# A two-layer decoder trunk in fp32: the output projection as seven block products instead of eight

## The reference, cut to what matters

```
h = rms_norm(x, norm1_g) * (1 + sc1) + sh1
y_a, y_b = two branches of h @ w_in (state-space mixer, latent attention)
merged = sigmoid(gate_a) * y_a + sigmoid(gate_b) * y_b
x = x + g1 * (merged @ w_out)              # the output projection: 1024 x 1024 x 1024
h = rms_norm(x, norm2_g) * (1 + sc2) + sh2
x = x + g2 * ((silu(h @ w_gate) * (h @ w_up)) @ w_down)
```

## Time and profile before

| what | us |
|---|---|
| median of 3 runs | 2896.54 (2896.39 to 2897.36) |
| the profiled execution | 2895.48 |
| its span, first to last instruction | 2893.6 |
| merge, layer 0 | 649 to 725 |
| output projection, layer 0 | 725 to 814 |
| down projection, layer 0 | 1247 to 1466 |

### The profile page before, as it was taken

How to read it: one execution, slowest core, us unless ns; L and a number is a source line. 1 busy time by engine, 2 the same in 40 slices (tenths; PEclk the granted TensorE clock), 3 DMA queues, 4 the chain that set the end, 5 groups by cost and what they waited for, 6 DMA issues and landing times.

```text
span 2893.6 us, 38026 instructions
## 1 busy us (share of the span) xinstructions
PE 2829.5 (98%) x13924; PEld 2386.9 (82%) x13924; DVE 2103.5 (73%) x2575; ACT 1223.9 (42%) x1965; POOL 1253.3 (43%) x834
## 2 busy tenths in 40 slices
PE   6999999999999999999999999999999899999998
PEld 6888889988877888888878888898888788888887
DVE  7998688865687777757668896788533878776665
ACT  3433377762242333344542335778313333233443
POOL 0354322242535555554625452223223555555454
PEclk9999999999999999999999999999999999999999
DMA  7565400224615544466635652011351345544665
GB/s 293 166 195 177 152 16 13 51 50 155 223 51 192 169 170 164 153 199 217 198 131 160 186 177 74 17 23 41 106 175 44 122 158 174 180 163 155 196 196 167
DMA packets 332745, 408.59 MB, mean 141 GB/s; under 512 B 52369, under 2 KB 242961, under 8 KB 328338
## 3 DMA queue, kind: packets, MB, share of 16 engines
q1 hardware_dynamic: 290128, 298.41, 34.0%
q10 hardware_dynamic: 42434, 107.77, 10.0%
HBM read 299.33 MB, written 104.40 MB: 140 GB/s over the span
## 4 chain that ended last, share of the span: by engine, by line
PE 86%; DVE 6%; ACT 3%; DMA 2%; POOL 1%; issue 1%; SPq 0%; ACTq 0%; DVEq 0%; POOLq 0%
PE ps L709 15%; PE ps L711 15%; PE ps L712 15%; PE ps L1775 9%; PE ps L1777 9%; PE ps L1776 9%; PE ps L1635 4%; PE ps L1616 2%; PE ps L1656 2%; PE ps L1655 2%; PE ps L1621 2%; PE ps L1620 2%; DMA raw<-in_w_b_out 1%; DVE h_lo L2581 1%; DMA ada_rows<-in_w_ada 1%
## 5 line engine op out<-in xcount | busy, mean ns | idle before, releaser
L655 POOL TENSOR_TENSOR wlo<-blocks,whi 128x512 fp32r<-128x512 f32 x288 | 430.3, 1501 | 378.0 <-ACT whi L649 375.2
L693 POOL TENSOR_TENSOR wlo<-raw,whi 128x1024 fp32r<-128x1024 f32 (+4 forms) x156 | 236.4, 1532 | 706.3 <-ACT whi L685 706.2
L649 ACT ACTIVATE whi<-blocks 128x512 fp32r<-128x512 f32 x288 | 180.4, 627 | 316.9 <-PE ps L1777 254.1
L2441 DVE TENSOR_TENSOR d_hi_lo<-blocks,d_hi_lo 128x512 fp32r<-128x512 f32 x154 | 204.3, 1330 | 140.7 <-ACT d_hi_lo L1912 140.4
L666 POOL TENSOR_TENSOR d_hi_lo<-w_pair,d_hi_lo 128x512 fp32r<-128x512 f32 x148 | 203.4, 1377 | 199.4 <-ACT d_hi_lo L1912 199.4
L709 PE MATMUL ps<-h_hi,whi 128*128 128x512 f32 x832 | 281.6, 401 | 7.0 <-DVE h_lo L2581 5.5
L711 PE MATMUL ps<-h_lo,whi 128*128 128x512 f32 x832 | 274.5, 393 | 0.0
L712 PE MATMUL ps<-h_hi,wlo 128*128 128x512 f32 x832 | 273.4, 391 | 0.0
L685 ACT ACTIVATE whi<-raw 128x1024 fp32r<-128x1024 f32 (+4 forms) x162 | 106.9, 699 | 353.0 <-PE ps L712 292.3
L1775 PE MATMUL ps<-h_hi,whi 128*128 128x512 f32 x640 | 249.5, 390 | 5.3 <-issue 3.2
L1777 PE MATMUL ps<-h_hi,wlo 128*128 128x512 f32 x640 | 249.1, 389 | 0.0
(11 more groups left out here) (338 smaller groups left out, 6888.4 us busy)
## 6 DMA issues: line engine op xcount, KB each, us to landing
blocks<-hidden_scratch SPq DMA_DIRECT2D x154, 256.0 KB, 3.7
ada_raw<-in_w_ada SPq DMA_DIRECT2D x64, 512.0 KB, 4.2
raw<-in_w_in SPq DMA_DIRECT2D x92, 256.0 KB, 4.6
w_pair<-in_w_down SPq DMA_DIRECT2D x22, 1024.0 KB, 6.2
sums_scratch<-w_pair ACTq DMA_DIRECT2D x22, 1024.0 KB, 3.9
w_pair<-sums_scratch SPq DMA_DIRECT2D x88, 256.0 KB, 3.3
blocks<-in_w_gate SPq DMA_DIRECT2D x84, 256.0 KB, 3.2
blocks<-in_w_up SPq DMA_DIRECT2D x84, 256.0 KB, 3.0
```

Of the source, the lines that this page charges most:

```text
L649: act.activation(block_view(whi, s), blocks[:, r, :], ACT.Copy).then_inc(block_hi.sem, 1)
L655: pool.tensor_tensor(block_view(wlo, s), blocks[:, r, :], block_view(whi, s).bitcast(F32), ALU.subtract)\
L693: last = pool.tensor_tensor(dst(wlo[:, s, :]), src(raw[:, s, :]), dst(whi[:, s, :].bitcast(F32)), ALU.subtract)
L2441: return dve.tensor_tensor(out, value, hi.bitcast(F32), ALU.subtract)
```

## The change

w_out and the merged input are cut into 2x2 blocks (four pairs of 128 rows, j = 0 to 3) and seven products P1 to P7 of sums of blocks give the result. There are 28 steps (n = 4 p + j, product p in the order P1, P5, P6, P3, P7, P2, P4), each of 4 x 3 matmuls into 4 PSUM banks; products alternate between banks 0 to 3 and 4 to 7. Four of them go on accumulating on what is left in their banks, and after every product DVE adds the 4 banks times g1 to x_sb (28 additions of 128x512 in all). High and low parts go through rings of three slots, as in the down projection. The sums of weight blocks (4 per pair, `weight_sums`) and of input blocks are made on DVE in the merge; w_out's pairs are loaded in its first four tiles. The squares' sum of half 0 is partly on DVE (k = 5 to 7). The 16 products for the modulation rows go into the down projection of layer 0, one every three steps, with their loads.

```diff
+    OPAIRS = KT // 2
+    OSTEPS = 7 * OPAIRS
+    OUT = ("P1", "P5", "P6", "P3", "P7", "P2", "P4")
+    OUT_BANK = {"P1": 0, "P6": 0, "P7": 0, "P4": 0, "P5": 4, "P3": 4, "P2": 4}
+    OUT_OPENS = ("P1", "P5", "P2")
...
# SP: w_out's pairs behind the gates of tiles 0 to 3; after the merge's last loads four plain blocks into raw
+                    if t < OPAIRS:
+                        load_out_pair(t)
...
+                for j in range(OPAIRS):
+                    if j % 2 == 0:
+                        sp.wait_ge(w_lo_done.sem, w_lo_done.at(l, U_MERGE + KT - 1 + j // 2))
+                        apart(sp)
+                    load_out_block(j, 0, 0, raw_part(j))
...
# SP, down projection
+                    if l + 1 < DEPTH and n % 3 == 0 and 0 <= n // 3 - 3 < 2 * KT:
+                        at = n // 3 - 3
+                        load_ada(l + 1, at // KT, at % KT, ada_used.at(l, 4 * KT + at - 1), next_raw)
...
# POOL
+                for n in range(OSTEPS):
+                    pool.wait_ge(wo_hi.sem, wo_hi.at(l, wo_hi_number(n, 0)))
+                    pool.tensor_tensor(ow_tile(n, 1), out_weight(n), ow_tile(n, 0).bitcast(F32), ALU.subtract)\
+                        .then_inc(wo_lo_w.sem, 1)
+                    if 21 <= n < 25:
+                        add_squares(l, 1, 0, n - 20)
+                    if n == 25:
+                        split_lo(pool, l, U_FFN)
+                split_lo(pool, l, U_FFN + 1)
+                for k in range(1, KT):
+                    add_squares(l, 1, 1, k)
...
# PE
+                    if j == 0:
+                        if p < 2:
+                            wait(pe, mg_free, l, KT - 1 + p)
+                        else:
+                            pe.wait_ge(wo_ev.sem, wo_ev.at(l, 4 * (p - 1)))
+                    pe.wait_ge(wo_lo_w.sem, wo_lo_w.at(l, n + 1))
...
+                        if n == 6 * OPAIRS and m == 1:
+                            pe.wait_ge(wo_ev.sem, wo_ev.at(l, 20 + 3))
+                            mean_squares(l, 2)
+                for n in range(OSTEPS):
+                    out_step(n)
+                    if n == 6 * OPAIRS:
+                        norm_scale(l, 2)
...
# ACT
+                def wo_hi_part(n):
+                    if n < OPAIRS:
+                        act.wait_ge(wo_loaded.sem, wo_loaded.at(l, 2 * 16 * OPAIRS))
+                        wait(act, unit_used, l, U_MERGE + KT - 1 + n // 2)
...
+                    else:
+                        act.wait_ge(wo_used.sem, wo_used.at(l, n - 2))
...
+                    copy(ow_tile(n, 0), out_weight(n)).then_inc(wo_hi.sem, 1)
+                    if n >= OPAIRS:
+                        copy(oh_tile(n, 0), out_hidden(n)).then_inc(wo_hi.sem, 1)
...
+                for n in range(2, 27):
+                    wo_hi_part(n)
+                    if 19 <= n < 23:
+                        out_square(0, n - 19)
+                    if n in (23, 24):
+                        for k in range(2):
+                            out_square(0, 2 * (n - 21) + k)
+                    if n == 25:
+                        split_hi(act, l, U_FFN)
                 norm_std(l, 2)
+                wo_hi_part(27)
...
# DVE
+                OUT_EVICTIONS = {8: ((0, 0), (0, 1)), 9: ((0, 2), (0, 3)), 11: ((1, 0),), 12: ((1, 1),), 13: ((1, 2), (1, 3)),
+                                 14: ((2, 0),), 15: ((2, 1),), 16: ((2, 2),), 17: ((2, 3),),
+                                 18: ((3, 0),), 19: ((3, 1),), 20: ((3, 2),), 21: ((3, 3),),
+                                 22: ((4, 0), (4, 1)), 23: ((4, 2), (4, 3))}
...
+                for n in range(OPAIRS, OSTEPS - 2):
+                    out_hidden_low(n)
+                    if n in (8, 11):
+                        wait(dve, x_back[n // 11], l, 16)
+                    for p, m in OUT_EVICTIONS.get(n, ()):
+                        out_eviction(p, m)
+                    if n == 24:
+                        squares_added(0, 5)
+                squares_added(0, 6)
+                squares_added(0, 7)
+                for m in range(4):
+                    out_eviction(5, m, True)
+                out_hidden_low(OSTEPS - 2)
                 norm_inverse(l, 2)
+                out_hidden_low(OSTEPS - 1)
...
+                for k in range(2):
                     hidden_lo(l, 2, k)
+                for m in range(4):
+                    out_eviction(6, m, True)
...
# DVE, down projection
+                    if l + 1 < DEPTH and n >= ADA_STEPS and n % 3 == 0 and n < ADA_STEPS + 6 * KT:
+                        at = (n - ADA_STEPS) // 3
+                        ada_product(l, 4 * KT + at, at // KT, next_raw, next_c)
```

More of the change, by code:

```diff
@@ L1112, in load_down_hidden @@
                     sp.dma_start(blocks[:, n % 4, :], hidden_dram[j, :, at, :]).then_inc(d_loaded[n % 4].sem, 16)
-                sp.wait_ge(s_max.sem, s_max.at(l, 16 * PAIRS))
-                apart(sp)
[L1116 to L1136, removed]
+                sp.wait_ge(wo_loaded.sem, wo_loaded.at(l, 16 * OPAIRS))
@@ new lines, in _ @@
+                sp.wait_ge(mg_comb.sem, mg_comb.at(l, 4 * OPAIRS))
+                apart(sp)
+                for j in range(OPAIRS):
+                    load_out_block(j, 1, 1, out_a22[j // 2][:, j % 2, :])
+                for n in range(2):
+                    sp.wait_ge(wo_lo_w.sem, wo_lo_w.at(l, 5 * OPAIRS + 2 * n + 2))
+                    apart(sp)
+                    up_unit(n)
+                sp.wait_ge(wo_lo_w.sem, wo_lo_w.at(l, 3 * OPAIRS + 4))
+                apart(sp)
+                for name in PLAIN_BLOCKS:
+                    load_block(name, 1)
@@ L1727, in _ @@
                     end[1].then_inc(unit_used.sem, 1)
[L1729 to L1749, removed]
@@ new lines, in out_square @@
+                def out_square(t, k):
+                    act.wait_ge(wo_ev.sem, wo_ev.at(l, (12, 20)[t] + k + 1))
+                    square(l, 1, t, k)
+                for t in range(KT):
+                    if t + 2 < KT:
+                        split_hi(act, l, U_MERGE + t + 2)
+                    if t % 2 == 0:
+                        act.wait_ge(mg_step.sem, mg_step.at(l, 2 * t + 2))
+                        copy(mg_hi[:, t // 2, :], m_sum[:, HALF:SEQ]).then_inc(mg_hi_done.sem, 1)
@@ L2243, in _ @@
+                table(ACT.Sqrt)
+                for n in range(2):
+                    wo_hi_part(n)
+                wait(act, unit_used, l, U_MERGE + KT)
                 wait(act, x_spilled, l, 16)
-                for part, tiles in enumerate((slice(0, 2), slice(2, KT))):
+                for part, tiles in enumerate((slice(0, 4), slice(4, KT))):
                     act.dma_start(x_sb[:, tiles, :], xs_dram[:, tiles, :]).then_inc(x_back[part].sem, 16)
-                for n in range(KT - 2):
-                    split_hi(act, l, U_OUT + n + 2)
-                    wait(act, wo_ev, l, n + 1)
-                    if n == 0:
-                        for part in x_back:
-                            wait(act, part, l, 16)
-                    for t in range(2):
-                        square(l, 1, t, n)
@@ L2255, in _ @@
-                for n in (KT - 2, KT - 1):
-                    wait(act, wo_ev, l, n + 1)
-                    square(l, 1, 0, n)
-                table(ACT.Sqrt)
-                norm_std(l, 2)
-                split_hi(act, l, U_FFN)
-                wait(act, wo_ev, l, KT + 1)
-                square(l, 1, 1, KT - 2)
-                for k in range(3):
-                    hidden_hi(l, 2, k)
-                split_hi(act, l, U_FFN + 1)
-                wait(act, wo_ev, l, KT + 2)
-                square(l, 1, 1, KT - 1)
@@ L2268, in _ @@
[L2268 to L2269 removed]
+                for n in range(2, 27):
+                    wo_hi_part(n)
+                    if 19 <= n < 23:
[5 more added lines that the diff above has]
+                        split_hi(act, l, U_FFN)
+                norm_std(l, 2)
+                wo_hi_part(27)
```

305 lines of the change are left out of this document (203 added, 102 removed).

## The result

The changed kernel takes **2927.55 us** (median of 4 runs, 2926.69 to 2928.93). The kernel before, run beside it, takes 2896.95 (2896.39 to 2900.53). The ratio is **1.0103**, with a 95% interval of 1.0086 to 1.0121: slower by about 1%, where 2921 and slower was forecast, with 2893 to 2934 as the range.

A forecast was written before the change was run, and what follows sets the result against it. PE was taken to bound the kernel, with feeding engines costing nothing if in time. Terms summed to +11.6 us a layer, with the rows 24.7 on 2895.48, and 1.06 for the median: 2921 us, range 2893 to 2934.

The forecast's parts named there:

- gain: Projection: 48 fewer matmuls a layer at 0.2267 us each, 10.9 us a layer saved on PE's path.
- start: Merge to projection: step 0 waits for loads, ACT's copy and POOL's subtraction; +1.5 us a layer (0.5 to 2.5).
- step 4: Projection's step 4 waits for DVE's list behind the last merge tile, colliding with POOL; +1.9 us a layer (0 to 3).
- evictions: Projection steps 8, 12, 16, 20 wait for DVE's evictions of the banks they add to; +5.1 us a layer.
- step 24: Projection: PE's sum of squares waits for squares, adds and P2's evictions; +10.1 us a layer (5.2 to 10.5).
- clock: After PE's idle time in step 24: lower granted clock; +0.9 us a layer (0 to 1.7).
- end: Projection's end to use of half 1's norm: four evictions, squares and adds remain; +3.0 us a layer (1 to 4.5).
- The modulation rows: Layer 0's down projection: 16 added DVE products make PE wait; +1.5 us, once (0 to 3.7).
- The loads: DMA share rises to about 0.8 in the merge and 0.9 in layer 0's down projection; no time cost.
- the first (no collisions): Feeding engines: all DVE operations take 0.68 us, remaining waits eat the gain; 2893 us, chance 0.12.
- the third (half of the wait): Step 24: POOL reaches its adds earlier, wait 5 for 10.1 us, no lost clock; 2909 us, chance 0.17.
- The second, that the gain arrives: Projection: the 28 steps run like the down projection, sum of squares waits under 2 us; 2879 us, chance 0.09.

The follow-up runs named there:

- y1_unit_between: Changed kernel with POOL's long low part of the next stage's first weights moved between weight parts 26 and 27; 2920.3 us, ratio 1.0080 to the kernel before.
- the reordered kernel: Changed kernel with DVE, POOL and ACT lists reordered, evictions and weight sums earlier, six adds a layer moved from POOL to DVE; 2880.9 us, ratio 0.9945.

## Why the prediction was right, term by term

The direction, the mechanism and its place were right; the total of one layer, +11.6, was 3.9 too small, and that of the program 24.7 for 33.5 on the span. Measured by distances of starts in layer 0:

| term | forecast | measured | from |
|---|---|---|---|
| gain | -10.9 | -10.9 | 13828 matmuls for 13924, 48 fewer a layer, at 0.2267 |
| start | +1.5 | +2.25 | 727.17 to 724.92 |
| step 4 | +1.9 | +1.9 | 12.81 - 10.88 |
| evictions | +5.1 | +4.8 | 12.38, 12.41, 11.76, 11.77, less 10.88 each |
| step 24 | +10.1 | +10.1 | 810.68 - (788.30 + 10.88 + 1.36) |
| clock | +0.9 | +2.8 | below |
| end | +3.0 | +4.5 | 15.54 - 11.01; 1.3 of it is the clock once more |

Their sum is 15.5, and 15.46 was measured. All rows but the gain and the clock are distances along one chain, so the agreement checks these two alone.

*Step 24* came as worked out, down to its parts. Behind the start of the step (799.36) the copies for step 25 were forecast at +2.4 and began at +2.35 (801.71). The low part was to end at +5.0 and ended at +4.9. The last add: +9.5, and +9.3. Two experiments take it apart. Moving POOL's long operation takes 2.15 us out of the wait, moving its adds 3.5, each as worked out beforehand.

*Evictions and step 4* were right in cause as well, since moving the evictions or the sums alone removes these waits. Step 4 was to cost 1.9 us by four operations that collide, of the seven between the last tile's sum and the low part; five did (1.67 to 1.78 each), since POOL's parts ended at 737.4 for 735.5. That the 1.9 agrees is luck: step 4 began at 739.98 for 739.2, and step 0, from which it is counted, at 727.17 for 726.4.

*The clock* was the largest mis-sized term. I took the 0.72 over 6 us of the earlier trace rows, behind a shorter pause. Here it was 0.52 over 5.8 us. The sum of squares took 1.72 us to the next start for 0.81 before, six matmuls 2.71 for 1.36, the norm 1.38 for 0.81: 0.9 + 1.35 + 0.6 = 2.8, above the upper end (1.7) that I had given. And I had the clock fall once; it fell again behind the wait for half 1's sum. From that sum to the norm's first use it took 4.95 us (835.14 to 840.09) at a granted 0.67, where y1_unit_between took 3.66 at 1.00 in its layer 0. These 1.3 us are in the row of the end, so the clock cost 4.1 us a layer for 0.9: this is the term that was mis-sized. The Trainium skill (TensorE: Matmul & The Clock Gate, "What's actually happening") has the clock fall with an idle PE: the trace agrees, since without the pause (squares left out) the sum in step 24 takes 1.05 again.

*The end* was at the upper bound (4.5); without the clock it is 3.2, for 3.0. POOL's six adds took 1.63 each (9.78), near the 1.77 taken. But the order of the turns there has two outcomes: the kernel with the long operation between parts 26 and 27 had an end of 13.0 us in one layer and of 15.0 in the other. Counted from the sum in step 24, the first use came 27.85 and 29.10 us later there, and 1.0 of these 1.25 is the clock between half 1's sum and the use (windows of that stretch in both layers, columns as in the earlier trace rows):

```profile
831.68:835.34 3.66, 3.65 (x24) 3.36 (x25) 2.14 (x4) 2.28 (x4) 0.00 (x0) 1.00 0.00 0
2260.35:2264.97 4.62, 4.62 (x23) 4.25 (x24) 2.23 (x4) 3.09 (x5) 0.00 (x0) 0.72 0.00 0
```

In the layer with the short end PE had waited 1.17 us for that sum, in the other 2.73. The changed kernel had the longer one in both layers of its profile, and the forecast, 14.0 by this measure (11.0 + 3.0), lies between. What decides the order of the turns was not settled; in that kernel P4's evictions waited 0.5 us for PE in the layer with the short end, and followed DVE's list without a pause in the other.

*The start*: the loads landed 5.3 us after issue (median), for 5.1 taken, but ACT's first copy began at 725.09 for 724.3. The merge itself ended 0.46 us later (724.93 to 724.47, the starts of its last matmuls), which I had not counted. Step 0 began at 726.22 and 726.94 in two profiles of the reordered kernel, so as much can come from the run.

*The modulation rows*: PE's waits in that stage were 0.16, 0.37, 0.28 and 0.43, 1.2 us in all, for 1.5 taken. By distances of starts, as in the table, it is more: from its first matmul to its last the stage took 216.72 us for 214.04, 2.7 longer, while in layer 1, which has no rows, it took 212.44 for 212.40. The nine other kernels with the same placement had 2.6 to 5.4, so the term was sized too low, and its range (0 to 3.7) too narrow.

*The loads*: where w_out's pairs came (650 to 690) the DMA share was 0.74 for about 0.8, and 0.48 before; in the down projection it was 0.79 for 0.9. PE waited for neither, as forecast.

The rest of the span's 33.5 us: 0.6 and 0.7 are regained between projection and down projection and 0.4 between layer 0's down projection and the end of layer 1's merge, and 1.8 is lost at the very end of the program, in the final norm. The last differs by 2.5 us between two profiles of the reordered kernel, so it is not put down to the change.

Of the rivals, the first (no collisions) falls by the halves and by the operation of 4 columns, and the third (half of the wait) by the 9.8. The second, that the gain arrives, was false for this order, but my argument against it was too strong: that 4 steps lie between a product and the next use of its banks, for 11 in the down projection, does not forbid it. The reordered lists run all 28 steps without a wait on the same ring.

## What to carry to other kernels

Before adding work to engines that feed PE, don't ask how busy they are but what stands behind what: write the lists for one step, with each operation of two SBUF operands on DVE and POOL as a turn as long as the other's operation, and see whether copies for the next step stand behind a result of this one. A move that removes a wait can give it back where the long operation then stands, so look at its new neighbours, small ones included. A wait of PE can cost more than its length: look at the granted clock behind each (2.8 us behind the wait of 9.8 here, 1.3 behind the one of 2.7). A saving on PE that does not show is worth a second try with the lists' order: here the same operations, in another order and with six adds a layer on another engine, went from 1.0% slower to 0.55% faster.

## What the runs showed of the hardware

- The size of the later operation did not matter for a turn: 2.36 us for an operation of 4 columns that takes 0.15 alone.
- Cutting POOL's operation in two shortened DVE's beside it (0.81 for 1.36) and the whole kernel (2919.9 for 2927.6, in part by its short end), though POOL then works 1.89 us a step for 1.29.
- Behind a pause of 10 us PE had 5.8 us at a granted clock of 0.52, busy in all of them: 2.8 us lost, for 1.7 behind the shorter pause of the earlier trace rows.
- Behind a wait of 2.73 us PE had 5.1 us at 0.67 (1.3 us lost); behind one of 1.17, with the same instructions following, the clock stayed at 1.00.
